# Attention heads in the middle of a unit: mixing of one head and scores of another move into a unit of matrix products, and two engines take up a new order

## The chip, the cores and the metric

The kernel runs on one core of a Trainium2 chip. The metric is the time of one execution on the device in microseconds (us), lower is better. Shown are the median of three runs and one execution taken by the hardware profiler.

The engines by their short names: PE is TensorE (matrix products; PEld is its loading of weights), DVE is VectorE, ACT is ScalarE, POOL is GpSimd, SP is SyncE, which here only issues DMAs. Each engine works off its own instructions in the order in which they are written, and waits on semaphores for the others.

## The reference

One token block of 512 positions with 1024 channels goes through a convolutional block with a gated feed-forward part, a retention layer with its feed-forward part, an attention layer, and a last feed-forward part. Only attention matters here: 16 heads of 64 channels. A chunk of 64 queries sees its own chunk and all earlier ones in the block (eight at most).

```python
def _chunk_attention(h, w_in, rel_bias, w_out):
    q, k, v = jnp.split(h @ w_in, 3, axis=-1)
    ...
        s = jnp.einsum('bqhd,bkhd->bhqk', qb, kb).astype(jnp.float32) * scale + bias[None]
        s = jnp.where(valid[None, None, None, :], s, -jnp.inf)
        p = jax.nn.softmax(s, axis=-1).astype(vb.dtype)
        return jnp.einsum('bhqk,bkhd->bqhd', p, vb)
    ...
    return o @ w_out
```

## The kernel before

**Units.** All big products are done in units of 24 matrix products (unit8, unit4, unit_v): each operand is split in a high and a low part, and a product is the sum of three (L686, L687, L688: high by high, low by high, high by low in some order). ACT makes the high part of weights (a half block at a time, L1200, in convert_half), POOL the low part (L665), SP loads the raw weights. A unit starts when its weights are ready (w_lo) and when its PSUM bank has been emptied (unit_taken); at its end it raises unit_done. In attention only banks 0 and 1 hold units (banks[0] = 2), since the others hold scores, turned probabilities and the mixture.

**The attention loop** runs over heads h = 1 to 15 on PE, ACT and DVE, each with its own copy of the loop. Queries, keys and values of four heads (a group) come from six units, done while other heads are worked on: qk_unit(0) to qk_unit(3) (queries and keys of two heads each) and two unit_v. With s = h % 4, head h has unit_v and qk_unit(0) at s = 1, qk_unit(1) at s = 2, qk_unit(2) at s = 3, qk_unit(3) and unit_v at s = 0. In the last group of heads (13 to 15, last_group) the units are parts of the output projection (unit4_narrow), which use both banks at a time.

**One head's way.** scores(h) on PE (L1057, L1059; four tiles of queries by their keys, in banks 2, 3 and 6) raises scores_done. maxima(h) on DVE adds the bias and takes row maxima (L2410), raising s_taken, then negates them (L2414). exps(h) on ACT (L1616) makes exponentials and row sums, and issues the DMA of the bias of h + 4 (load_bias). normalise(h) on DVE (L2418, L2423) divides, raising p_ready. turn(h) on PE (L1075) transposes ten blocks of probabilities into banks 4, 5 and 6; bank 6 also holds a tile of scores, so its two blocks wait until maxima(h + 1) have read it. probs_hi(h) on ACT (L1625) and probs_lo(h) on DVE (L2429) take the high and low parts, raising pt_ready. mix(h) on PE (L1086, L1088) multiplies by the values into bank 7; it waits for pt_ready of its own head and for mix_added of the head before. mixed_copy and mixed_hi on ACT (L1631, L1636), mixed_add and mixed_lo on DVE (L2434, L2440) bring the mixture into two parts for the output projection. The last tile of scores(h) waits for pt_ready of head h - 2, whose turned blocks stood in bank 6.

**Queries and keys.** After a qk_unit DVE scales it (qk_taken, L2006), ACT takes the high part (qk_hi, L1580 and L1581), DVE the low part (qk_lo, L2400). ACT then converts some halves of weights (qk_done: one, none, two, one for the four units) and, for keys, issues two DMAs that copy the high part to the other half of the partitions (copy_k_hi, L1587), for which its queue first waits for its own high part. SP does the same for the low part.

**Order.** It is written out by hand for each engine and each s. On PE, at s = 1, 2 and 3: the unit, scores(h + 1), mix(h - 1), turn(h); at s = 0: qk_unit(3), unit_v, scores(h + 1), mix(h - 1), turn(h). On ACT and DVE the work on the unit comes first, that on head h + 1 next, the parts of head h behind it.

Of the kernel before, what the change touches and what calls it, by code (L numbers as in the profile page):

```python
# [26 lines left out]
D = 1024  # L27
# [137 lines left out]
def build(nc, phases, x_in, w_in, w_out, w_gate, w_up, w_down, ret_w_in, ret_w_out, att_w_in,  # L165
# [4 lines left out]
    with ctx:  # L170
# [45 lines left out]
        sq, sq_end, so_far = cols[:, 32:36], cols[:, 36:40], cols[:, 40:44]  # L216
# [463 lines left out]
        def _(pe):  # L680
# [36 lines left out]
            def unit4(rhs, k0, ready=None, fresh=1, bank0=None, last=None):  # L717
# [7 lines left out]
                for m, k in [(m, k) for tiles in ((0, 1, 2), (3,)) for m in range(2) for k in tiles]:  # L725
                    if ready and m == 0:
                        pe.wait_ge(ready, c.next(ready))
# [194 lines left out]
            for f in phases:  # L922
# [107 lines left out]
                if f == "att":  # L1030
# [7 lines left out]
                    def unit4_narrow(n):  # L1038

                        unit4(H, 0, fresh=0, bank0=0)  # L1040
# [64 lines left out]
                    for h in range(1, ATT_HEADS):  # L1105
                        s, last_group = h % 4, h >= ATT_HEADS - 4
                        if s == 0:
                            qk_unit(3)
                            unit_v(X)
                            scores(h + 1)  # L1110
                            mix(h - 1)
                            turn(h)
                            continue
# [3 lines left out]
                        if last_group and s == 1:  # L1117
                            scores(h + 1)
                            pe.wait_ge(mix_ready, 8)
                            unit4_narrow(s - 1)  # L1120
                        else:
                            if last_group:
                                unit4_narrow(s - 1)
                            else:
                                qk_unit(s - 1)
                            if h + 1 < ATT_HEADS:
                                scores(h + 1)
                        if s == 1:
                            pe.wait_ge(unit_taken, v_units)
                        mix(h - 1)  # L1130
# [12 lines left out]
        def _(act):  # L1143
# [224 lines left out]
            for f in phases:  # L1368
# [197 lines left out]
                if f == "att":  # L1566
# [89 lines left out]
                    for h in range(1, ATT_HEADS):  # L1656
                        s, last_group = h % 4, h >= ATT_HEADS - 4
                        if s == 0:
                            qk_unit(3)
                            mixed_copy(h - 1)  # L1660
                            v_unit(0)
                            exps(h + 1)
# [5 lines left out]
                        if last_group and s == 1:  # L1668
                            exps(h + 1)
                            after_unit()  # L1670
                            mixed_copy(h - 1)
                        else:
                            if last_group:
                                after_unit()
                            else:
                                qk_unit(s - 1)
                            mixed_copy(h - 1)
                            if h + 1 < ATT_HEADS:
                                exps(h + 1)
                        probs_hi()  # L1680
# [12 lines left out]
        def _(dve):  # L1693
# [207 lines left out]
            def end_rows(u):  # L1901
# [10 lines left out]
                if u == 12:  # L1912
                    ended(1, right)
                    dve.wait_ge(squared, 4)
                    V.tensor_scalar(so_far[:, 2:4], sq[:, 2:4], 1.0 / D, EPS, ALU.mult, ALU.add).then_inc(dve_step, c.made(dve_step))
                    dve.wait_ge(dve_step, c.now(dve_step))
                if u in (12, 13):
# [4 lines left out]
                    V.tensor_scalar(ms[:, p:p + 1], sq_end[:, p:p + 1], 1.0 / D, so_far[:, p:p + 1], ALU.mult, ALU.add).then_inc(  # L1922
# [114 lines left out]
            for f in phases:  # L2037
# [333 lines left out]
                if f == "att":  # L2371
# [99 lines left out]
                    for h in range(1, ATT_HEADS):  # L2471
                        s, last_group = h % 4, h >= ATT_HEADS - 4
                        if s == 0:
# [3 lines left out]
                            mixed_add(h - 1)  # L2477
                            value_lo()
                            normalise(h + 1)
# [5 lines left out]
                        if last_group and s == 1:  # L2485
                            maxima(h + 1)
                            out_narrow(s - 1)
                            mixed_add(h - 1)
                            normalise(h + 1)
                        elif last_group:  # L2490
                            out_narrow(s - 1)
                            if h + 1 < ATT_HEADS:
                                maxima(h + 1)
                            mixed_add(h - 1)
                            if h + 1 < ATT_HEADS:
# [72 lines left out]
```

## Time and profile before

| | |
|---|---|
| median of three runs | 1866.5 us (1863.9 to 1867.17) |
| the profiled execution | 1866.14 us, its span 1864.3 us |
| PE busy | 1841.6 us, 99% |
| DVE, POOL, ACT busy | 1133.3 us (61%), 944.8 us (51%), 843.2 us (45%) |
| attention loop, heads 1 to 15 | 1315.6 to about 1499 us of the span |
| mean granted clock of PE | 0.997 of full speed |

The span goes from the first to the last instruction. A timeline line gives start, duration, engine and line; x10 means ten instructions merged; a bracket gives the idle time in front of it and what ended it. The durations of PE's products overlap, since they are pipelined: the time that one takes of the engine is the distance to the next start, 0.23 us for 512 columns and 0.12 us for 256.

### The profile page before, as it was taken

How to read it: one execution, taken by the hardware profiler on the slowest of the kernel's cores; microseconds unless marked ns; L12 is line 12 of the kernel's file. 1: busy time of each engine (PE TensorE's matmuls, PEld its weight loads, DVE VectorE, ACT ScalarE, POOL GpSimd, SP SyncE). 2: the span in 40 equal slices, each digit the busy share in tenths (PEclk: the TensorE clock that was granted, in tenths of full speed). 3: DMA queues.
4: the chain of work that ended last, by engine and by line, in shares of the span. 5: the costliest groups of instructions: out<-in, count | busy, mean ns of one | idle time of the engine just before them, and what ended most of it. 6: DMA issues, size and time to landing. Idle time of an engine off the chain costs nothing.

```text
span 1864.3 us, 24027 instructions
## 1 busy us (share of the span) xinstructions
PE 1841.6 (99%) x9444; PEld 1570.6 (84%) x9444; DVE 1133.3 (61%) x1816; ACT 843.2 (45%) x1318; POOL 944.8 (51%) x407
## 2 busy tenths in 40 slices
PE   8999999999999999999999999999999999999998
PEld 7778889898888888888889898998888887888886
DVE  6987775775776333343565445457777766454546
ACT  5335443343354233332454445355666646443544
POOL 5673466475443433333448566574222327674755
PEclk9999999999999999999999999999999999999999
DMA  5222414424232222222243232403333332423221
GB/s 186 91 91 68 140 64 141 158 69 158 73 113 68 91 91 87 72 91 90 75 174 114 68 136 67 137 25 100 98 103 111 103 98 83 136 76 127 91 91 57
DMA packets 142764, 187.10 MB, mean 100 GB/s; under 512 B 4000, under 2 KB 102576, under 8 KB 142528
## 3 DMA queue, kind: packets, MB, share of 16 engines
q1 hardware_dynamic: 134848, 171.72, 27.9%
q10 hardware_dynamic: 7808, 13.91, 2.6%
q8 instruction: 72, 1.18, 0.3%
q14 instruction: 36, 0.29, 0.0%
HBM read 179.28 MB, written 6.33 MB: 100 GB/s over the span
## 4 chain that ended last, share of the span: by engine, by line
PE 81%; DVE 8%; ACT 3%; POOL 1%; issue 1%; ACTq 0%; DVEq 0%
PE ps L686 26%; PE ps L687 26%; PE ps L688 26%; DVE ps L2068 1%; POOL w_lo L665 1%; ACT w_hi L1200 1%; DVE diagonals L1736 1%; DVE xl L1762 0%; ACT work L1616 0%; DVE probs_t_lo L2429 0%; PE ps L1075 0%; DVE work L2423 0%; PE ps L1009 0%; DVE work L2410 0%; DVE work L2006 0%
## 5 line engine op out<-in xcount | busy, mean ns | idle before, releaser
L665 POOL TENSOR_TENSOR w_lo<-raw,w_hi 128x1024 fp32r<-128x1024 f32 x244 | 590.9, 2430 | 755.5 <-ACT w_hi L1200 755.4
L686 PE MATMUL ps<-xh,w_hi 128*128 128x512 f32 x1408 | 555.1, 394 | 5.7 <-DVE xl L1762 3.5
L688 PE MATMUL ps<-xh,w_lo 128*128 128x512 f32 x1408 | 549.3, 390 | 0.0
L687 PE MATMUL ps<-xl,w_hi 128*128 128x512 f32 x1408 | 549.1, 390 | 0.0
L1200 ACT ACTIVATE w_hi<-raw 128x1024 fp32r<-128x1024 f32 x262 | 273.2, 1057 | 426.3 <-PE ps L688 397.6
L686 PEld LDWEIGHTS ps<-xh,w_hi 128*128 128x128 f32 x1408 | 265.0, 188 | 65.0 <-issue 10.1
L687 PEld LDWEIGHTS ps<-xl,w_hi 128*128 128x128 f32 x1408 | 265.1, 188 | 55.5 <-issue 1.9
L688 PEld LDWEIGHTS ps<-xh,w_lo 128*128 128x128 f32 x1408 | 264.9, 188 | 55.5
L686 PE MATMUL ps<-hid_hi,w_hi 128*128 128x256 f32 (+1 forms) x688 | 228.4, 332 | 1.5 <-DVE hid_lo L2012 0.7
L688 PE MATMUL ps<-hid_hi,w_lo 128*128 128x256 f32 (+1 forms) x688 | 227.1, 330 | 0.0
L687 PE MATMUL ps<-hid_lo,w_hi 128*128 128x256 f32 (+1 forms) x688 | 227.1, 330 | 0.0
L686 PEld LDWEIGHTS ps<-hid_hi,w_hi 128*128 128x128 f32 x688 | 130.8, 190 | 14.6 <-DVE hid_lo L2012 1.8
L688 PEld LDWEIGHTS ps<-hid_hi,w_lo 128*128 128x128 f32 x688 | 130.8, 190 | 12.1
L687 PEld LDWEIGHTS ps<-hid_lo,w_hi 128*128 128x128 f32 x688 | 130.9, 190 | 11.7 <-issue 0.2
L665 POOL TENSOR_TENSOR w_lo<-down,w_hi 128x1024 fp32r<-128x1024 f32 x40 | 96.2, 2420 | 84.0 <-ACT w_hi L1200 84.0
L1977 DVE TENSOR_TENSOR x<-x,ps 128x512 f32<-128x512 f32 x84 | 56.9, 684 | 75.5 <-PE ps L688 75.5
L665 POOL TENSOR_TENSOR w_lo<-work,w_hi 128x1024 fp32r<-128x1024 f32 x36 | 86.3, 2413 | 13.0 <-ACT w_hi L1200 13.0
L2344 DVE SCALAR_TENSOR_TENSOR work<-ps,r_bc 128x512 f32<-128x512 f32 x64 | 43.6, 689 | 79.6 <-PE ps L688 79.6
L686 PE MATMUL ps<-w_hi,xh 128*128 128x512 f32 (+1 forms) x256 | 86.6, 338 | 0.7 <-DVE work L2229 0.7
L687 PE MATMUL ps<-w_lo,xh 128*128 128x512 f32 (+1 forms) x256 | 86.0, 336 | 0.0
L688 PE MATMUL ps<-w_hi,xl 128*128 128x512 f32 (+1 forms) x256 | 86.0, 336 | 0.0
L688 PE MATMUL ps<-combined,w_lo 128*128 128x256 f32 x288 | 81.5, 283 | 0.0
(272 smaller groups left out, 3095.0 us busy)
## 6 DMA issues: line engine op xcount, KB each, us to landing
raw<-in_mlp_w_dram SPq DMA_DIRECT2D x40, 1024.0 KB, 5.5
raw<-in_ret_w_in_dram SPq DMA_DIRECT2D x24, 1024.0 KB, 5.2
work<-in_mlp_w_dram SPq DMA_DIRECT2D x16, 1024.0 KB, 5.7
raw<-in_att_w_in_dram SPq DMA_DIRECT2D x12, 1024.0 KB, 5.3
raw<-in_w_gate_dram SPq DMA_DIRECT2D x11, 1024.0 KB, 5.3
raw<-in_w_up_dram SPq DMA_DIRECT2D x11, 1024.0 KB, 5.4
raw<-in_w_in_dram SPq DMA_DIRECT2D x9, 1024.0 KB, 5.1
raw<-in_ret_w_out_dram SPq DMA_DIRECT2D x8, 1024.0 KB, 5.0
```

The lines of the kernel that those rows point to most:

```text
L665: nc.gpsimd.tensor_tensor(half_of(wl[:, b % 2, :], b, half), half_of(source, b, half), half_of(wh[:, b % 2, :], b, half).bitcast(F32), ALU ...
L686: nc.tensor.matmul(o, a[0], b[0], start=first, stop=False, skip_group_check=True)
L687: nc.tensor.matmul(o, a[0], b[1], start=False, stop=False, skip_group_check=True)
L688: return nc.tensor.matmul(o, a[1], b[0], start=False, stop=last, skip_group_check=True)
L1200: nc.scalar.activation(to, source, ACT.Copy).then_inc(w_hi, c.made(w_hi))
L1736: V.reciprocal(rough, root_rows).then_inc(dve_step, c.made(dve_step))
L1977: V.tensor_tensor(tiles, tiles, ps[:, where, :].rearrange("p (m c) -> p m c", m=2), ALU.add).then_inc(unit_taken, c.made(unit_taken))
L2068: V.scalar_tensor_tensor(total if last else acc, src, w, acc, ALU.mult, ALU.add).then_inc(signal, c.made(signal))
L2344: V.scalar_tensor_tensor(hval[:, u % 2, :], bank(), 0.0, r_bc[:, :], ALU.max, ALU.mult).then_inc(unit_taken, c.made(unit_taken))
```

## The change

- unit4 and unit4_narrow take a function that is called in the middle of the unit, as unit8 has already. It is called ahead of the fifth of eight triples of products.
- PE: at s = 1, 2 and 3, mix(h - 1) goes into the middle of the unit, and so does scores(h + 1) at s = 1 (except in the last group) and s = 2, behind mix. At s = 3 scores(h + 1) stays behind the unit. At s = 0 mix(h - 1) and scores(h + 1), now in this order, go between qk_unit(3) and unit_v.
- ACT: mixed_copy(h - 1) goes first. Exponentials of h + 1 go ahead of the work on the unit at s = 1 and 2; at s = 1 probs_hi(h) too goes ahead of it. At s = 0 the exponentials go ahead of the values' part. The last group gets a corresponding order.
- DVE: at s = 1 and 2, maxima(h + 1) and mixed_add(h - 1) go ahead of qk_taken, and probs_lo(h) ahead of normalise(h + 1). At s = 3 the order is mixed_add, qk_taken, maxima, qk_lo, normalise, probs_lo. At s = 0 normalise(h + 1) goes ahead of value_lo.
- A name of a small tile (so_far) becomes sq_half; its three places are left out below.

```diff
@@ -714,7 +714,7 @@
                 mm.then_inc(unit_done, c.made(unit_done))
                 c.unit.n += 1
 
-            def unit4(rhs, k0, ready=None, fresh=1, bank0=None, last=None):
+            def unit4(rhs, k0, ready=None, fresh=1, bank0=None, last=None, between=None):
 
                 slot, half = c.unit.n // 2 % 2, c.unit.n % 2
                 pe.wait_ge(w_lo, low(1))
@@ -723,6 +723,8 @@
                 w = weights(slot, 512)
 
                 for m, k in [(m, k) for tiles in ((0, 1, 2), (3,)) for m in range(2) for k in tiles]:
+                    if between and (m, k) == (1, 1):
+                        between()
                     if ready and m == 0:
                         pe.wait_ge(ready, c.next(ready))
                     if last and (m, k) == (0, 3):
@@ -1035,9 +1037,9 @@
                         slot0 = (c.unit.n - n) // 2 % 2
                         unit8(X, slot=(slot0 + n % 2) % 2, half=n // 2, ahead=(1, 2, 0, 1)[n], between=between)
 
-                    def unit4_narrow(n):
-
-                        unit4(H, 0, fresh=0, bank0=0)
+                    def unit4_narrow(n, between=None):
+
+                        unit4(H, 0, fresh=0, bank0=0, between=between)
 
                     def scores(h):
 
@@ -1106,9 +1108,9 @@
                         s, last_group = h % 4, h >= ATT_HEADS - 4
                         if s == 0:
                             qk_unit(3)
+                            mix(h - 1)
+                            scores(h + 1)
                             unit_v(X)
-                            scores(h + 1)
-                            mix(h - 1)
                             turn(h)
                             continue
                         if s == 1 and h > 1:
@@ -1116,18 +1118,21 @@
                             v_units = c.unit.n
                         if last_group and s == 1:
                             scores(h + 1)
+
+                        def inside():
+                            if s == 1:
+                                pe.wait_ge(unit_taken, v_units)
+                            mix(h - 1)
+                            if s == 2 or s == 1 and not last_group:
+                                scores(h + 1)
+
+                        if last_group:
                             pe.wait_ge(mix_ready, 8)
-                            unit4_narrow(s - 1)
+                            unit4_narrow(s - 1, inside)
                         else:
-                            if last_group:
-                                unit4_narrow(s - 1)
-                            else:
-                                qk_unit(s - 1)
-                            if h + 1 < ATT_HEADS:
+                            qk_unit(s - 1, inside)
+                            if s == 3:
                                 scores(h + 1)
-                        if s == 1:
-                            pe.wait_ge(unit_taken, v_units)
-                        mix(h - 1)
                         turn(h)
                     unit4_narrow(3)
                     mix(ATT_HEADS - 1)
@@ -1658,26 +1663,31 @@
                         if s == 0:
                             qk_unit(3)
                             mixed_copy(h - 1)
+                            exps(h + 1)
                             v_unit(0)
-                            exps(h + 1)
                             probs_hi()
                             mixed_hi(h - 1)
                             continue
                         if s == 1 and h > 1:
                             v_unit(1)
-                        if last_group and s == 1:
+                        if last_group:
+                            if s == 1:
+                                exps(h + 1)
+                            mixed_copy(h - 1)
+                            if s == 2:
+                                exps(h + 1)
+                            after_unit()
+                            probs_hi()
+                        else:
+                            mixed_copy(h - 1)
+                            if s == 3:
+                                qk_unit(2)
                             exps(h + 1)
-                            after_unit()
-                            mixed_copy(h - 1)
-                        else:
-                            if last_group:
-                                after_unit()
-                            else:
-                                qk_unit(s - 1)
-                            mixed_copy(h - 1)
-                            if h + 1 < ATT_HEADS:
-                                exps(h + 1)
-                        probs_hi()
+                            if s == 2:
+                                qk_unit(1)
+                            probs_hi()
+                            if s == 1:
+                                qk_unit(0)
                         mixed_hi(h - 1)
                     after_unit()
                     mixed_copy(ATT_HEADS - 1)
@@ -2475,35 +2485,40 @@
                             maxima(h + 1)
                             qk_lo(3)
                             mixed_add(h - 1)
+                            normalise(h + 1)
                             value_lo()
-                            normalise(h + 1)
                             probs_lo()
                             mixed_lo(h - 1)
                             continue
                         if s == 1 and h > 1:
                             value_lo()
-                        if last_group and s == 1:
-                            maxima(h + 1)
-                            out_narrow(s - 1)
-                            mixed_add(h - 1)
-                            normalise(h + 1)
-                        elif last_group:
-                            out_narrow(s - 1)
-                            if h + 1 < ATT_HEADS:
+                        if last_group:
+                            if s < 3:
                                 maxima(h + 1)
                             mixed_add(h - 1)
-                            if h + 1 < ATT_HEADS:
+                            if s == 1:
                                 normalise(h + 1)
+                            out_narrow(s - 1)
+                            probs_lo()
+                            if s == 2:
+                                normalise(h + 1)
+                        elif s == 3:
+                            mixed_add(h - 1)
+                            qk_taken(2)
+                            maxima(h + 1)
+                            qk_lo(2)
+                            normalise(h + 1)
+                            probs_lo()
                         else:
+                            maxima(h + 1)
+                            mixed_add(h - 1)
                             qk_taken(s - 1)
-                            maxima(h + 1)
                             if s == 2:
-                                qk_lo(s - 1)
-                            mixed_add(h - 1)
-                            if s != 2:
-                                qk_lo(s - 1)
+                                qk_lo(1)
+                            probs_lo()
                             normalise(h + 1)
-                        probs_lo()
+                            if s == 1:
+                                qk_lo(0)
                         mixed_lo(h - 1)
                     out_narrow(3)
                     mixed_add(ATT_HEADS - 1)
```

## Rows read from the trace of the kernel before

**Rows 1.** The page, part 1: busy us, share of the span, instructions.

```profile
PE 1841.6 (99%) x9444; PEld 1570.6 (84%) x9444; DVE 1133.3 (61%) x1816; ACT 843.2 (45%) x1318; POOL 944.8 (51%) x407
```

**Rows 2.** Waits of PE, 1315 to 1500 us: total, times, longest.

```profile
PE ps L1075 <- DVE cols L2410: 2.4, 7, 0.5
PE ps L1057 <- DVE probs_t_lo L2429: 0.7, 2, 0.4
```

**Rows 3.** Timeline of PE: start, us, operation [idle before it, and releaser].

```profile
1321.13 0.22 PE L1057 MATMUL ps<-k_parts,q_hi 128*128 128x128 f32 x1
...
1322.63 0.38 PE L1057 MATMUL ps<-k_parts,q_hi 128*128 128x256 f32 x1 [0.30 <-DVE probs_t_lo L2429]
...
1322.97 0.40 PE L1086 MATMUL ps<-probs_t_hi,att_v 128*128 128x512 f32 x1
...
1324.20 1.28 PE L1075 MATMUL ps<-ident,work 128*128 128x128 f32 x10
1325.23 0.47 PE L686 MATMUL ps<-xh,w_hi 128*128 128x512 f32 x1
...
1330.80 0.22 PE L1057 MATMUL ps<-k_odd,q_lo 128*128 128x128 f32 x1
...
1350.99 0.28 PE L686 MATMUL ps<-w_hi,xh 128*128 128x256 f32 x1
...
1356.75 0.22 PE L1057 MATMUL ps<-k_odd,q_lo 128*128 128x128 f32 x1
```

**Rows 4.** Timeline of ACT, 1322 to 1336 us.

```profile
1323.21 0.63 ACT L1580 ACTIVATE q_hi<-work 64x512 fp32r<-64x512 f32 x1 [2.45 <-DVE work L2006]
...
1324.51 1.06 ACT L1200 ACTIVATE w_hi<-raw 128x1024 fp32r<-128x1024 f32 x1
1325.59 0.59 ACT L1631 ACTIVATE work<-ps 64x512 f32<-64x512 f32 x1
...
1328.32 0.19 ACT L1616 ACTIVATION_READ_ACCUMULATOR work<-work,cols 128x1 f32 x1
1328.53 1.36 ACT L1625 ACTIVATE probs_t_hi<-ps 128x512 fp32r<-128x512 f32 x3
...
1335.47 0.62 ACTq L1587 DMA_DIRECT2D k_odd<-k_odd  x1
```

**Rows 5.** Timeline of DVE, 1320 to 1333 us.

```profile
1320.97 1.61 DVE L2429 TENSOR_TENSOR probs_t_lo<-ps,probs_t_hi 128x512 fp32r<-128x512 f32 x3
1322.50 0.68 DVE L2006 SCALAR_TENSOR_TENSOR work<-ps,r_bc 128x512 f32<-128x512 f32 x1
1323.10 0.28 DVE L2410 CUSTOM_DVE_ANT_0 work<-ps,work 128x128 f32<-128x128 f32 x1
...
1324.85 0.17 DVE L2414 TENSOR_SCALAR cols<-cols 128x4 f32<-128x4 f32 x1
1326.22 0.68 DVE L2434 TENSOR_TENSOR work<-ps,work 64x512 f32<-64x512 f32 x1 [1.20 <-ACT work L1631]
1326.93 1.67 DVE L2400 TENSOR_TENSOR q_hi<-work,q_hi 64x512 fp32r<-64x512 f32 x1
1328.63 0.69 DVE L2400 TENSOR_TENSOR q_lo<-work,q_lo 64x512 fp32r<-64x512 f32 x1
...
1329.57 1.28 DVE L2423 TENSOR_SCALAR work<-work,cols 128x128 f32<-128x128 f32 x4
1330.76 1.61 DVE L2429 TENSOR_TENSOR probs_t_lo<-ps,probs_t_hi 128x512 fp32r<-128x512 f32 x3
```

**Rows 6.** Timeline of POOL, 1320 to 1330 us.

```profile
1325.64 2.42 POOL L665 TENSOR_TENSOR w_lo<-raw,w_hi 128x1024 fp32r<-128x1024 f32 x1 [6.10 <-ACT w_hi L1200]
```

**Rows 7.** Two stretches: length, busy us by engine, granted clock, DMA, GB/s.

```profile
core 0: us, PE busy (x) PEld busy (x) DVE busy (x) ACT busy (x) POOL busy (x), PEclk, DMA share, GB/s
8.41:15.24 6.83, 5.45 (x13) 4.20 (x14) 4.32 (x6) 6.06 (x11) 4.14 (x3) 0.50 0.99 333
1855.00:1858.40 3.40, 1.78 (x8) 1.13 (x6) 2.87 (x10) 1.28 (x4) 0.00 (x0) 1.00 0.55 223
```

**Rows 8.** Timeline of PE, 6 to 11 us.

```profile
9.79 0.77 PE L686 MATMUL ps<-xh,w_hi 128*128 128x512 f32 x1 [3.51 <-DVE xl L1762]
```

More of the change, by code:

```diff
@@ L215, in build @@
         mv = cols[:, 24:32].rearrange("p (i c) -> p i c", c=2)
-        sq, sq_end, so_far = cols[:, 32:36], cols[:, 36:40], cols[:, 40:44]
+        sq, sq_end, sq_half = cols[:, 32:36], cols[:, 36:40], cols[:, 40:44]
         mx, nmx, rs, rinv = (cols[:, 32 + 4 * k:36 + 4 * k] for k in range(4))
@@ L1914, in end_rows @@
                     dve.wait_ge(squared, 4)
-                    V.tensor_scalar(so_far[:, 2:4], sq[:, 2:4], 1.0 / D, EPS, ALU.mult, ALU.add).then_inc(dve_step, c.made(dve_step))
+                    V.tensor_scalar(sq_half[:, 2:4], sq[:, 2:4], 1.0 / D, EPS, ALU.mult, ALU.add).then_inc(dve_step, c.made(dve_step))
                     dve.wait_ge(dve_step, c.now(dve_step))
@@ L1921, in end_rows @@
                     dve.wait_ge(squared, p + 3)
-                    V.tensor_scalar(ms[:, p:p + 1], sq_end[:, p:p + 1], 1.0 / D, so_far[:, p:p + 1], ALU.mult, ALU.add).then_inc(
+                    V.tensor_scalar(ms[:, p:p + 1], sq_end[:, p:p + 1], 1.0 / D, sq_half[:, p:p + 1], ALU.mult, ALU.add).then_inc(
                         to_curve, c.made(to_curve))
```

## The prediction, made before the change was run

> **What bounds the kernel now.** I read the page first, then the waits of TensorE (PE), then the timelines of the four engines over one head of attention. PE is busy for 99% of the span [rows 1]. So nothing can be gained by doing other engines' work faster. What can be gained or lost is PE's idle time. The attention loop runs from 1315.6 to about 1499 us. In its wait table the longest kinds are the turning products L1075 waiting for the last row maximum (2.4 us, 7 times) and the last score product L1057 waiting for low parts of the probabilities (0.7 us, 2 times) [rows 2]. The table counts idle from a modelled end, which lies 0.17 us after the time at which the next product could have started, so each of these waits costs that much more: the 0.30 us before the product at 1322.63 is a gap of 0.47 between starts [rows 3]. Summed over the 15 such gaps from 1315 to 1499 us I get about 6.5 us. That is all that any reordering of this loop can win: 0.35% of the time.
>
> **Who feeds PE.** Head h goes through this ring: scores (PE), maxima (DVE), exponentials (ACT), normalising (DVE), turning (PE), high part (ACT), low part (DVE), mixing (PE). In the kernel before, a whole unit of other products stands between turning head h-1 and the first need of its low parts. I call the first half of a unit H. A unit with its ten turning products takes 6.60 us (1324.20 to 1330.80), and turning alone about 1.06, so a unit is 5.5 us and H is 2.73. A values' unit takes 5.76 (1350.99 to 1356.75). Scores take 1.3 to 1.4 undisturbed (1.84 from 1321.13 to 1322.97 less the gap; I use 1.27, as where nothing waits), mixing 1.23 (1322.97 to 1324.20) [rows 3].
> Even with the whole unit the cover is thin: turning of head 1 ends at 1325.23, its low parts are done at 1332.37 (1330.76 plus 1.61), 7.1 us later [rows 3, 5].
>
> **What the change does to that cover.** Mixing of h-1 moves from behind the unit (and behind the scores) into its middle. It now comes H, 2.73 us, after turning of h-1, where it came 5.5 + 1.3 = 6.8 us after it. The low parts took 7.1 us. So the new order on ACT and DVE must bring them forward by 4.4 us. Whether it does must be laid out head by head, with these durations. ACT [rows 4]: exponentials of a head 2.3 (from the end of the mixture's copy at 1326.18 to 1328.51), high parts 1.36, a part of queries or keys 1.3 (1323.21 to 1324.51, two of 0.63), a converted half of weights 1.0 (1.06 with its tail), copy of the mixture 0.6, and on keys' units 1.2 in which ACT's queue issues two DMAs of about 0.6 each and lets nothing pass (the second from 1335.47 to 1336.09). DVE [rows 5]: maxima 1.75 and their negation 0.17, normalising 1.4 with its reciprocal, low parts 1.55, scaling a unit 0.62, a low part of queries or keys two times 0.70, sum of the mixture 0.7. PE to the next engine and back cost 0.05 to 0.2 each.
>
> **The lock between POOL and DVE.** The low part of the queries at 1326.93 takes 1.67 us where the next, of the same form, takes 0.69. POOL ran its product of weights from 1325.64 to 1328.06, and the DVE instruction ended 0.54 us after that [rows 5, 6]. So an instruction of DVE that reads SBUF alone waits out a POOL instruction of 2.4 us; those that read PSUM (scaling, maxima, low parts) don't. I use this for normalising and for the low parts of queries and keys. The Trainium skill ("SBUF — State Buffer", section "SBUF: two separate sides") states it as an exclusive lock of the shared port pair, held for the whole instruction; by that rule normalising is locked out too, which no row of mine shows at full length. Without any lock the layout below comes to +16.7 us, with it to +27.7.
>
> **The layout.** I put the four queues in the order of the code with these numbers. As a test I did it first for the kernel before: mixing of head 15 ends at 1498.4 by the layout and at about 1499 in the trace, with 7.7 us of stalls where the gaps give 6.5. For the changed order, zero at the end of turning of a head with h%4 = 1:
> - h%4 = 2. PE: H to 2.7; mixing finds its low parts (DVE done at 2.5), no wait; scores to 5.2, second half to 8.0. DVE: low parts to 2.5, normalising to 3.9, low part of queries: one half to 4.6, then POOL has the port (4.6 to 7.0), other half to 7.7, low part of the mixture to 8.35. Only then come the maxima of h+1, whose scores were there at 5: 8.35 to 10.1. The last two turning products wait for them: 1.3 us. Turning ends at 10.3.
> - h%4 = 3. ACT: exponentials 10.3 to 12.6, then, ahead of the turned parts, keys' part to 13.9 and its DMA issues to 15.0, high parts to 16.4. DVE: low parts at 17.2. PE wanted them at 10.3 + 2.7 = 13.1: a stall of 4.2 us. Then mixing, half, scores to 22.5, and 0.5 us for the maxima; turning ends at 24.0.
> - h%4 = 0. ACT: queries' part to 23.4, two converted halves to 25.4, exponentials to 27.6, high parts to 29.0. POOL holds the port from 27.8 to 30.1. DVE: normalising to 31.3 and only behind it low parts to 32.9. PE has done its unit at 29.5: a stall of 3.5 us. Before, a values' unit and the scores stood here too, another 7 us of cover.
> - h%4 = 1. A values' unit and H lie between: no wait.
> Per group of four heads 1.3 + 4.2 + 0.5 + 3.5 = 9.5 us, three groups 28 (the first 0.4 less). Head 1: mixing of head 0 now comes at 1318.1, its low parts, whose order is untouched, at 1322.58 [rows 5]: 4.5. Last group, narrow units: 2.9, since each waits for both banks of the one before. In all 35.4 against 7.7 laid out for before: **+27.7 us**. The gaps that the change is to close (maxima before turning, scores before low parts) are in that sum: they shrink or vanish in places, and cost more at h%4 = 2.
> Exchanging names (so_far) costs nothing. No instruction is added. SP's queue keeps its order; its waits on the low parts of keys come a few us later in a group of now 58, and each load had over 10 us in hand. The POOL queue also keeps its order.
>
> **The clock.** All of the loop runs at full level. In this trace PE idled once for as long as these stalls: 3.51 us before the product at 9.79 [rows 8]. Around it the granted clock is 0.50 (1.2 GHz) from 8.41 to 15.24 us, with 5.45 us of PE work in it [rows 7]; at full level that is half, so the fall cost 2.7 us. At the end of the kernel, in a stretch in which PE worked 1.78 of 3.40 us, it stayed at 1.00 [rows 7]. The long stalls laid out above, 3.5 to 4.5 us, are thus of the one length ahead of which a fall is on record. I price one fall from nothing (it comes at the end of a stall and part of it is taken up by the next stall) to 2.7 us, and take 2 us, nearer to the row. All eight would give about +14 (two of them are half taken up), four give +8.
> The Trainium skill ("TensorE: Matmul & The Clock Gate", "Why this matters for your kernels") likewise warns of idle gaps between bursts of products. By its words all stalls of this length are at risk; the trace has the one case, and the sum needs only that.
>
> **The rivals.**
> - A, forecast: the stalls come and the clock falls at about half of the long ones: 1866.1 + 27.7 + 8 = 1902, from 1896 to 1909. Chance 0.55.
> - B: the stalls come, the clock holds: 1893.8. For it: each stall hardly exceeds the one seen. Chance 0.22.
> - C: POOL's lock doesn't hit normalising and the keys' parts where I put it: +16.7, so 1883 with the clock held. For it: the order of POOL and DVE hangs on tenths. Against: low parts of queries are hit in every group before. Chance 0.10.
> - D, the other side: ACT and DVE do bring the low parts within 2.73 us of turning, so mixing never waits, and the maxima are ready for turning. Then up to 6.5 us are won: 1860. The point from which it decides is ACT's: exponentials of the next head must be done before turning begins, at h%4 = 3 too. At h%4 = 1 to 2 this holds; at 3 the keys' part and 1.17 us of DMA issues stand ahead of the high parts. Chance 0.07.
> - E: the waits only change places and the sum stays within 0.2% of before, about 1866. That would also be so if the halves inside a unit did not cut as the code says. Chance 0.04.
> - More than A's upper end (all falls, each at 2.7 us, or other engines slowed too): 0.02.
>
> **Numbers.** All sums start from the profiled run, 1866.14 us, of which 1864.3 is span; it is 0.4 below the median of three, 1866.5, so the forecast needs no shift. 1883 to 1911 holds A, B and C, and leaves out D, E and a little above. 0.2%, 3.7 us, is about what a measurement of this kernel can tell from no change. Faster by more: D, 0.07. Within: E, 0.04. Slower by more: the rest, 0.89.
>
> **What would show it.** In the profile after: L1086 (mixing) appears as a waiter for DVE's low parts L2429 (by its new number), with some 25 us in all and single waits of 3.5 to 4.5; the wait of L1075 for maxima stays near 1 us at h%4 = 2; the loop from head 1 to head 15 lengthens by 28 to 42 us and nothing outside it; the granted clock has stretches of 0.50 behind long stalls. Rival B shows the same waits and a clock of 1.00, C waits near 2 us, D none on L1086. I am wrong in the mechanism if PE never waits for L2429 in the middle of a unit, and wrong in size if the stall at h%4 = 0 is missing, because normalising got the port first.

## The result, and the profile after

The changed kernel takes 1908.2 us (median; 1905.5 to 1909.1) against 1866.8 of the kernel before on the same chip: a ratio of 1.0225, 95% interval 1.0212 to 1.0237. The profiled execution took 1909.05 us (span 1907.3), 42.9 us more than the profiled one before.

The page of the kernel after, busy time and the granted clock over 40 slices (compare [rows 1]):

```profile
PE 1858.0 (97%) x9444; PEld 1583.8 (83%) x9444; DVE 1142.4 (60%) x1816; ACT 841.9 (44%) x1318; POOL 946.5 (50%) x407
PEclk9999999999999999999999999999899999999999
```

PE has the same 9444 instructions, but 16.4 us more busy time: some of them ran slower. The one 8 in the clock's row, the slice from 1478 to 1526 us, points at one such place; the others hardly show in slices of 47.7 us. Idle and slower work are two separate losses, and each has its own view.

Waits of PE in the kernel after, 1300 to 1550 us, total, times, longest (compare [rows 2]):

```profile
PE ps L1088 <- DVE probs_t_lo L2439: 24.8, 7, 4.2
PE ps L1077 <- DVE cols L2420: 3.2, 7, 0.7
PE ps L686 <- DVE x L2459: 1.8, 4, 0.8
PE ps L686 <- DVE att_v L2393: 0.7, 1, 0.7
```

A new first row: mixing (now L1088) waits seven times for low parts of the probabilities. The sum is 30.5 us in 19 waits; with 0.17 us for each, as in the prediction, 33.7. Before it was 6.5, so the stalls cost **27.2 us**. Turning still waits for the maxima seven times, 3.2 us in all where it was 2.4.

Timeline of PE after, the instructions behind a stall of over 0.3 us in the first group of heads (compare [rows 3]):

```profile
1323.25 0.62 PE L1088 MATMUL ps<-probs_t_hi,att_v 128*128 128x512 f32 x1 [4.16 <-DVE probs_t_lo L2439]
...
1340.88 0.44 PE L1077 MATMUL ps<-ident,work 128*128 128x128 f32 x2 [0.52 <-DVE cols L2420]
...
1348.18 0.77 PE L1088 MATMUL ps<-probs_t_hi,att_v 128*128 128x512 f32 x1 [4.10 <-DVE probs_t_lo L2439]
...
1357.71 0.44 PE L1077 MATMUL ps<-ident,work 128*128 128x128 f32 x2 [0.36 <-DVE cols L2420]
...
1366.41 0.47 PE L1088 MATMUL ps<-probs_t_hi,att_v 128*128 128x512 f32 x1 [2.78 <-DVE probs_t_lo L2439]
```

These are head 1, then h%4 = 2, 3 and 0. The pattern comes back at 1409 and 1428, and at 1471 and 1487.

Why it waits at 1348.18 (ACT, then DVE, kernel after): exponentials end at 1343.3, keys' part and its DMA issues follow, and only then the high parts of the turned probabilities.

```profile
1343.27 0.61 ACT L1585 ACTIVATE k_parts<-work 64x512 fp32r<-64x512 f32 x1
1343.89 0.63 ACT L1586 ACTIVATE k_odd<-work 64x512 fp32r<-64x512 f32 x1
1344.60 0.48 ACTq L1592 DMA_DIRECT2D k_parts<-k_parts  x1
1345.12 0.62 ACTq L1592 DMA_DIRECT2D k_odd<-k_odd  x1
1345.78 1.36 ACT L1630 ACTIVATE probs_t_hi<-ps 128x512 fp32r<-128x512 f32 x3 [1.27 <-issue]
...
1346.41 1.62 DVE L2439 TENSOR_TENSOR probs_t_lo<-ps,probs_t_hi 128x512 fp32r<-128x512 f32 x3 [0.46 <-ACT probs_t_hi L1630]
...
1348.15 1.27 DVE L2433 TENSOR_SCALAR work<-work,cols 128x128 f32<-128x128 f32 x4
```

And at 1366.41 (POOL, ACT, DVE): the high parts began at 1361.47 and took 1.36 us, but DVE normalises first, and that takes 3.04 us here where it takes 1.27 in the row above, with POOL busy from 1358.40 to 1363.66.

```profile
1358.40 5.26 POOL L665 TENSOR_TENSOR w_lo<-raw,w_hi 128x1024 fp32r<-128x1024 f32 x2 [20.48 <-ACT w_hi L1205]
...
1361.47 1.36 ACT L1630 ACTIVATE probs_t_hi<-ps 128x512 fp32r<-128x512 f32 x3
...
1361.69 3.04 DVE L2433 TENSOR_SCALAR work<-work,cols 128x128 f32<-128x128 f32 x4
1364.66 1.61 DVE L2439 TENSOR_TENSOR probs_t_lo<-ps,probs_t_hi 128x512 fp32r<-128x512 f32 x3
```

The second loss. The seven stretches of the loop of the kernel after in which the granted clock is 0.50 (columns as in [rows 7]), the first, second and last of them and the sum of all seven:

```profile
1323.40:1326.81 3.41, 3.41 (x13) 3.22 (x14) 0.00 (x0) 0.59 (x1) 0.00 (x0) 0.50 0.35 118
1347.30:1354.13 6.83, 5.95 (x17) 5.01 (x18) 3.46 (x9) 1.09 (x2) 0.00 (x0) 0.50 0.16 38
...
1487.25:1494.08 6.83, 6.63 (x25) 6.27 (x26) 3.92 (x14) 3.58 (x7) 2.38 (x1) 0.50 0.17 40
sum 34.12, PE 32.00 PEld 28.93 DVE 17.18 ACT 11.65 POOL 5.05; mean PE 4.57 PEld 4.13 DVE 2.45 ACT 1.66 POOL 0.72
```

Each begins within 1.5 us of the end of one of the seven long stalls. PE did 32.0 us of work in them, which takes half as long at the full level: **16.0 us** lost. 27.2 + 16.0 = 43.2, against 42.9 measured.

### The profile page after: what moved, and what is told of

It is laid out like the page before. It is cut to its first block, busy times and chain, and to the rows that moved or that the text cites. A ratio compares the mean times of both kernels' runs of the same rounds, so it can differ in the third digit from the quotient of the medians.

```text
span 1907.3 us, 24027 instructions
## 1 busy us (share of the span) xinstructions
PE 1858.0 (97%) x9444; PEld 1583.8 (83%) x9444; DVE 1142.4 (60%) x1816; ACT 841.9 (44%) x1318; POOL 946.5 (50%) x407
## 4 chain that ended last, share of the span: by engine, by line
PE 79%; DVE 9%; ACT 4%; issue 2%; POOL 1%; ACTq 0%; DVEq 0%
PE ps L686 25%; PE ps L687 25%; PE ps L688 25%; DVE ps L2078 1%; ACT work L1621 1%; POOL w_lo L665 1%; ACT w_hi L1205 1%; DVE probs_t_lo L2439 1%; DVE work L2420 1%; DVE work L2433 1%; PE ps L1088 1%; DVE diagonals L1746 1%; PE ps L1090 1%; DVE xl L1772 0%; PE ps L1011 0%
```

## The experiments

The theory: the low parts come late for three separate reasons (ACT's order at h%4 = 3, DVE's order and POOL at h%4 = 0, the untouched order of head 0), and each long stall costs its length and a fall of the clock. The rivals: the clock's part is something else, such as slower products by conflicts; POOL's hold on DVE doesn't matter; the loss is the work of one engine's order alone.

**1. Fill the stalls.** Ahead of mixing's wait PE does unused products; the operands and the other engines' orders stay.

```diff
+FILL = {0: 14, 2: 14, 6: 14, 10: 14, 3: 10, 7: 10, 11: 10}
...
+                        for _ in range(FILL.get(h, 0)):
+                            nc.tensor.matmul(ps[:, 7, :], X[0][:, 0, 0:P], X[0][:, 0, :], start=True, stop=True, skip_group_check=True)
```

> The changed kernel with 14 or 10 products of 512 columns (0.2275 us each) put ahead of the wait for low parts at the seven long stalls (mixing of heads 0, 2, 6, 10: 14; of 3, 7, 11: 10). They write into the mixture's bank, which the next product overwrites, and stand in time that PE would have idled. Theory (stalls by waits for DVE 27.7 us, and a lower clock behind each): no stretch at half level in the loop, waits of L1088 fall to about 1 us each, the waits of DVE and ACT stay where they are, time 1866.8 + 27.7 = 1894.5, from 1892 to 1897; so the clock's part is 14 us. Rival (the half level is a mere sign of the stalls and costs nothing, since other engines end last there): the clock is full and the time stays at 1908. Second rival (PE's speed does not matter and the filling gets in the way): over 1908.

Measured: 1894.3 us, ratio 1.0150 (1.0133 to 1.0167). Waits of PE in this kernel, 1300 to 1550 us, then its stretch from 1315 to 1500 us, which is most of the loop, then the same stretch of the kernel after:

```profile
PE ps L1091 <- DVE probs_t_lo L2442: 4.8, 7, 0.9
```

```profile
1315.00:1500.00 185.00, 176.10 (x1026) 153.23 (x1025) 137.74 (x306) 103.01 (x233) 49.75 (x20) 1.00 0.28 84
```

```profile
1315.00:1500.00 185.00, 156.97 (x849) 137.01 (x847) 126.97 (x283) 94.87 (x216) 45.50 (x18) 0.91 0.28 82
```

The clock stays at 1.00, where it was 0.91, and no stretch of the loop is at half level. Late data cost as much as before, since the fill only takes the place of idle time, but 13.9 us are gone. That is the clock's part, net; what is left over the kernel before, 27.9 us, is the stalls' part.

**2 to 4. Undo two causes, one by one and together.** In the second, at h%4 = 2 (where the low parts that mixing will want at h%4 = 3 are made), the parts of h go ahead of the keys' part on ACT and DVE. In the third, at h%4 = 3, DVE's low parts go ahead of normalising.

```diff
@@ second: ACT, then DVE (s = 2)
-                            if s == 2:
-                                qk_unit(1)
                             probs_hi()
-                            if s == 1:
-                                qk_unit(0)
+                            if s < 3:
+                                qk_unit(s - 1)
...
+                            probs_lo()
                             if s == 2:
                                 qk_lo(1)
-                            probs_lo()
@@ third: DVE (s = 3)
-                            normalise(h + 1)
                             probs_lo()
+                            normalise(h + 1)
```

> The changed kernel, with the high parts of the turned probabilities ahead of the keys' part and its DMA issues on ACT at h%4 = 2, and the low parts ahead of the keys' low part on DVE. Theory (the stall at h%4 = 3 is ACT's 1.3 us of keys' part and 1.2 us of DMA issues ahead of the high parts): each of the three stalls there falls from 4.2 to about 1.7 us, turning at h%4 = 3 waits 0.4 more, stalls in all -6 us, and three falls of the clock go too: 1908.2 - 6 - 5 = 1897, from 1893 to 1901. Rival (the exponentials of the next head alone set it, the rest is hidden): stalls stay at 4.2 and the time at 1908.

> The changed kernel, with the low parts ahead of normalising on DVE at h%4 = 3. Theory (the stall at h%4 = 0 is DVE's normalising ahead of the low parts, held up by POOL's hold on the port): the three stalls of 2.9 us there fall to under 0.5, their three falls of the clock go, 1908.2 - 9 - 5 = 1894, from 1890 to 1898. Rival (ACT's high parts, behind two conversions and the exponentials, set it): the stalls stay above 2 us, the time falls by less than 3 us.

> Both edits. Theory: the savings add up; left over are the stall of head 1 (4.5 us, with a fall of the clock), three of 1.7 us at h%4 = 3 and those for the maxima: 12.3 us over the kernel before by stalls, 14 with the clock: 1881, from 1877 to 1885. Rival (one stall's time is only handed to the next): not below 1890.

Measured: 1899.3 us (1.0178; 1.0161 to 1.0195), 1894.5 (1.0154; 1.0137 to 1.0171), and both 1884.9 (1.0099; 1.0083 to 1.0116). The stall that each takes away, in the timelines of PE of the second and of the third:

```profile
1345.75 0.47 PE L1088 MATMUL ps<-probs_t_hi,att_v 128*128 128x512 f32 x1 [1.71 <-DVE probs_t_lo L2437]
```

```profile
1362.36 0.47 PE L1088 MATMUL ps<-probs_t_hi,att_v 128*128 128x512 f32 x1 [0.27 <-DVE probs_t_lo L2439]
```

4.10 became 1.71, and 2.78 became 0.27. With the stalls went most of the falls: seven in the kernel after, five in the second (one of them behind the 1.71 us shown), four in the third, and one with both. The two gains, 8.9 and 13.7 us, add up to 22.6, and together they gave 23.3. With both, though, 1885 was at the slow end of what was expected (1877 to 1885), and the timeline shows two waits in the first group that neither edit alone leaves (what makes them was not followed up):

```profile
1352.32 0.30 PE L1059 MATMUL ps<-k_parts,q_hi 128*128 128x128 f32 x1 [1.00 <-issue]
...
1362.53 0.47 PE L1088 MATMUL ps<-probs_t_hi,att_v 128*128 128x512 f32 x1 [1.57 <-DVE probs_t_lo L2437]
```

**5 and 6. Take POOL's hold away.** In the kernel after (5) and in the one before (6), POOL makes the low part of the attention weights for one of eight blocks of columns only; seven eighths of these low parts are left out, PE's work is the same.

```diff
+                    low, source, high = [half_of(t, b, half) for t in (wl[:, b % 2, :], source, wh[:, b % 2, :])]
+                    if in_att:
+                        low, source, high = [t[:, 0:1, :] for t in (low, source, high)]
```

> The changed kernel with POOL's low parts of the weights of queries, keys and values in attention cut to one of 8 rows of blocks (a product over 128 instead of 1024 columns), so those low parts are left out for seven eighths and POOL holds the port for some tenths of a us instead of 2.4. Theory (POOL's hold on the port of DVE is what delays the maxima at h%4 = 2 and normalising at h%4 = 0): the waits for maxima vanish at h%4 = 2, the stalls at h%4 = 0 fall from 2.9 to about 1.2, those at h%4 = 3 from 4.2 to about 2.7; head 1 stays. 12 us over the kernel before by stalls, and fewer falls of the clock: 1883, from 1878 to 1890. Rival (DVE's long instructions have another cause, POOL runs beside them by chance): times as in the changed kernel, 1908, or over 1900.

> The same cut in the kernel before, as the measure for the run above. Theory: the waits for low parts at heads 1 and 2 and for the maxima get shorter: 1866.4 - 4.5 = 1862, from 1860 to 1865. Rival (no hold on the port): 1866 as before.

Measured: 1882.8 us (1.0094; 1.0079 to 1.0110) and 1860.2 (0.9973; 0.9962 to 0.9984). In the fifth, POOL's instruction and the waits of PE (total, times, longest):

```profile
1358.36 0.46 POOL L669 TENSOR_TENSOR w_lo<-raw,w_hi 128x128 fp32r<-128x128 f32 x1 [8.36 <-ACT w_hi L1207]
```

```profile
PE ps L1090 <- DVE probs_t_lo L2441: 13.9, 7, 2.9
```

So the change costs 22.6 us where POOL's instructions are short, and 41.3 where each takes 2.4 us. Nearly half of the loss is late orders meeting POOL. Three falls were left.

Head 1 was expected to stay and did not: its stall fell from 4.16 to 2.47 us. Ahead of the low parts of head 0, for which that mixing waits, stand the maxima, exponentials and normalising of head 1, and the negation of these maxima takes 1.82 us in the kernel after, beside POOL (1315.32 to 1320.05 us), and 0.17 in the fifth run:

```profile
1315.90 1.82 DVE L2424 TENSOR_SCALAR cols<-cols 128x4 f32<-128x4 f32 x1
...
1312.93 0.17 DVE L2426 TENSOR_SCALAR cols<-cols 128x4 f32<-128x4 f32 x1
```

So the third of the causes named above is in part POOL's hold too.

**7 and 8. One side of the change alone.** Seven: the new order of ACT and DVE with PE's old one. Eight: PE's new order with the old one of ACT and DVE. The core of each, against the kernel after:

```diff
@@ seven: PE
-                            mix(h - 1)
-                            scores(h + 1)
                             unit_v(X)
+                            scores(h + 1)
+                            mix(h - 1)
...
-                            qk_unit(s - 1, inside)
+                                qk_unit(s - 1)
...
+                        mix(h - 1)
@@ eight: ACT
+                                qk_unit(s - 1)
...
-                            exps(h + 1)
-                            if s == 2:
-                                qk_unit(1)
-                            probs_hi()
-                            if s == 1:
-                                qk_unit(0)
+                                exps(h + 1)
+                        probs_hi()
```

> The new order of ACT and DVE with TensorE's order of the kernel before: the whole unit and the scores stand again between turning and mixing. Nothing of the computation is left out. Layout: the low parts still come late by the rows of the changed kernel (keys' part and its DMA issues ahead of the high parts at h%4 = 3, normalising ahead of the low parts at h%4 = 0), but now the cover is longer, so the long waits of mixing for low parts go; in their place the maxima come late (waits of up to 3 us of turning at h%4 = 2 and 3) because the unit's own scaling and parts come in another order than PE delivers. Sum of stalls by layout +27.5 us, and two or three falls of the clock: 1894 to 1898 us. Rival, that only TensorE's order matters and ACT's and DVE's order is an improvement on any order of TensorE: 1866 or less.

> The kernel before with PE's new order alone; ACT and DVE keep their old order. Theory (the new order on ACT and DVE does bring the low parts forward, only not enough): now 13 to 14 long stalls of 1.7 to 4.5 us, at h%4 = 2 too, since exponentials and normalising stand ahead of the low parts at every head; 55 us by stalls and some 12 to 20 by the clock: 1935, from 1920 to 1945. Rival (the reordering of ACT and DVE is what hurts, PE's is harmless): below 1885.

Measured: seven 1902.9 us (1.0202; 1.0187 to 1.0218), eight 1944.9 (1.0423; 1.0407 to 1.0439). Waits of PE in seven, then in eight, 1300 to 1550 us:

```profile
PE ps L1077 <- DVE cols L2417: 17.1, 7, 2.9
PE ps L686 <- DVE x L2456: 8.9, 4, 5.2
```

```profile
PE ps L1088 <- DVE probs_t_lo L2434: 39.9, 10, 4.5
PE ps L1077 <- DVE cols L2415: 11.1, 10, 1.6
```

Neither half is harmless: +37 and +79 us. With the old order on ACT and DVE, PE's new one stalls in most heads; the new order on ACT and DVE brings the waits for low parts from 39.9 to 24.8 us and those for maxima from 11.1 to 3.2 (to the end of the eighth run's longer loop they are 43.0 and 13.2). By itself, beside PE's old order, it makes the maxima late. Seven was expected at 1894 to 1898. Its stalls are as laid out (26.9 us by the gaps, laid out 27.5); its clock fell seven times and not two or three, and cost some 10 us (11.6 by the windows). Eight ended at the upper end of its 1920 to 1945, for the same reason: its stalls are 56.0 us by the gaps, laid out 55, but the clock fell eleven times and cost 23.6 us by the windows, where 12 to 20 were expected.

**9. A better order by the layout.** A search over the orders, costed with the same durations, gave this one (PE keeps the whole unit before mixing at h%4 = 1 to 3 and splits the values' unit at h%4 = 0; letters are the steps: t scaling, x maxima, ma sum of the mixture, q low parts of the unit, w values' part, ml its low part, n normalising, p low parts):

```diff
+DVE_STEPS = {0: 't x ma q w ml n p'.split(), 1: 'w x p ma t n ml q'.split(), 2: 't x ma q n ml p'.split(), 3: 't x ma q p ml n'.split()}
```

> An order that keeps a whole unit between turning of a head and its mixing, and uses the middle of a unit only where low parts have had 5.5 us: at h%4 = 0 mixing and scores in the middle of the values' unit; scores inside or behind as before elsewhere, at h%4 = 2 behind mixing. On ACT and DVE the parts of head h go ahead of the exponentials and the normalising of h+1 at h%4 = 1, 3. Theory (PE's idle time of 6.5 us in the loop is all there is to win): the waits left are 0.7 at head 1, 0.5 three times for the maxima and 0.6 for the first narrow unit: 1866.4 - 5 = 1861.4, from 1860 to 1864. Rival (PE's gaps are a fixed cost of its semaphores, and go nowhere): 1866.

Measured: 1870.7 us (1.0028; 1.0017 to 1.0038), a miss by 9 us, to the other side. POOL, DVE and PE of this kernel:

```profile
1332.67 2.39 POOL L669 TENSOR_TENSOR w_lo<-raw,w_hi 128x1024 fp32r<-128x1024 f32 x1 [11.83 <-ACT w_hi L1211]
...
1332.00 0.69 DVE L2400 TENSOR_TENSOR q_hi<-work,q_hi 64x512 fp32r<-64x512 f32 x1
1332.72 2.89 DVE L2400 TENSOR_TENSOR q_lo<-work,q_lo 64x512 fp32r<-64x512 f32 x1
...
1338.03 0.69 PE L1083 MATMUL ps<-ident,work 128*128 128x128 f32 x2 [2.35 <-DVE cols L2410]
```

POOL started 0.05 us before DVE's second low part, in the gap between two DVE instructions; that one took 2.89 us instead of 0.69, the maxima came late, and turning waited 2.35 us. The same happened in all three groups (POOL ahead by 0.05 or 0.06 us each time), and behind the first of them the clock fell once. The layout, which gave the maxima 0.5 us, did not have this hold.

**10. A robust order.** PE: mixing ahead of scores at h%4 = 2, both inside the values' unit at h%4 = 0, otherwise as before. DVE: low parts ahead of normalising in every head before the last group. ACT: high parts ahead of exponentials only at h%4 = 2. The copy of the mixture at h%4 = 2 and 3 and the values' low part at h%4 = 0 change places too. It was chosen as the one whose sum stays good when single durations are moved by tenths.

```diff
-                            unit_v(X)
-                            scores(h + 1)
-                            mix(h - 1)
+                            unit_v(X, both)
...
+                            if s == 2 and not last_group:
+                                mix(h - 1)
```

> TensorE keeps the order of the kernel before, but for mixing ahead of scores at h%4 = 2, and mixing and scores in the middle of the values' unit at h%4 = 0. DVE takes the low parts of the probabilities ahead of normalising in every head, ACT takes the high parts ahead of exponentials at h%4 = 2 only. Nothing of the computation is left out. Layout: 3.5 us less of stalls than in the kernel before (2.3 to 4.4 when single durations are moved by tenths), with no stall over 1.1 us and so no fall of the clock: 1862.8 us, from 1861.5 to 1864.5. Rival, that such orders hang on tenths in which POOL and DVE take the port and that the layout can't see them (as in the run e9_parts_first): a wait of 2 us for the maxima in each group, 1866 to 1872.

Measured: 1862.3 us, ratio 0.9983 (0.9974 to 0.9992): the one full version that beats both kernels, by 0.17%. Its maxima before turning:

```profile
PE ps L1077 <- DVE cols L2425: 1.5, 4, 0.5
```

Four waits are left of the seven of [rows 2]. No stretch of the loop has a half clock. Its profiled execution (1864.4 us) shows only 1.7 us of the gain, the medians 3.9; the interval (1.5 to 4.9 us) holds both.

**11. The ninth with short POOL products** (the same seven eighths of low parts left out; the edit is that of 5), to test what was said of the ninth.

> The order of e9_parts_first, with POOL's low parts of the attention weights taken over 128 of 1024 columns, so that this part of the weights' low parts is left out of the computation. If the 10 us by which e9_parts_first missed its layout are POOL holding the port in front of DVE's second low part of the queries, they go: 1861 us (1859 to 1863), the waits of turning L1083 for the maxima fall from 7.4 us to under 2 us, and no stretch of the loop has a half clock. The kernel before with the same short products took 1860.2. Rival, that the 2.4 us waits come from the order itself: 1868 to 1871 with the waits still there.

Measured: 1861.5 us (0.9972; 0.9962 to 0.9982). Waits of PE:

```profile
PE ps L1085 <- DVE cols L2412: 1.6, 4, 0.4
```

Of the 7.4 us that turning waited in the ninth, 1.6 are left: the rest was POOL. And both orders, the old one (1860.2) and this one, are then 1.3 us apart, to the old one's side: this order has no gain of its own.

## Why the prediction was right, and where it was not

It said 1902.0 us, from 1883 to 1911; the median is 1908.2. The case that came is A, stalls and falls of the clock, within its own range (1896 to 1909).

- **What bounds the kernel.** Right. PE's idle time (27.2) and its time at half clock (16.0), both inside the loop, are all of the 42.9 us.
- **The cover** of 2.73 us instead of 6.8 before the low parts are wanted: right, as the first row of the waits after and the eighth run show.
- **The layout**, as gaps (bracket plus 0.17), predicted and measured: head 1 4.5 and 4.33; h%4 = 3 4.2 and 4.27; h%4 = 0 3.5 and 2.95; maxima at h%4 = 3 0.5 and 0.53; last group 2.9 and 3.4 (1.8 and 0.7 us in five waits). Too high: the maxima at h%4 = 2, 1.3 against 0.69 (0.88 in the second group). Sum +27.7 predicted, +27.2 from the waits, +27.9 from the first experiment. That the sum is this close is partly luck: the layout had 35.4 for 33.7 us after and 7.7 for 6.5 before, and the two errors cancel. The loop lengthened by 43.0 us (the first product behind mixing of head 15 starts at 1499.25 and 1542.24), a little over the 28 to 42 named, and nothing outside it did.
- **The stall at h%4 = 0** was laid out 0.5 us too long. The half clock is not the reason: in the first experiment, all at full level, PE does unused products from 1360.00 on and mixing starts at 1362.88, so the stall is 2.88 us there too.

```profile
1360.00 2.43 PE L1086 MATMUL ps<-xh 128*128 128x512 f32 x10
...
1362.88 0.50 PE L1091 MATMUL ps<-probs_t_hi,att_v 128*128 128x512 f32 x1 [0.45 <-DVE probs_t_lo L2442]
```

  What differs first is POOL: in the layout it holds the port until 6.1 us after the end of turning and the low parts are done at 8.9; in the kernel after, where turning ends at 1357.90, POOL ends at 5.8 and the low parts at 8.4.
- **POOL and DVE.** This was the assumption without a full-length row, and rival C was its absence. The normalising of 3.04 us is that row, and the fifth and sixth runs price all of POOL's holds together: without them the change costs 22.6 us, near C's 16.7 plus three falls (the gaps of the two runs differ by 16.3). The hold at head 1, 1.82 against 0.17 us, was not seen in the prediction; it got the stall right because it took that time from the trace of before, where it is as long. The Trainium skill ("SBUF — State Buffer", section "SBUF: two separate sides") has the port pair held for a whole instruction; these rows agree, 2.89 us of DVE against 2.39 of POOL in the ninth run.
- **The clock: the term that was mis-sized.** The prediction took four falls at 2 us, +8. There were seven, one behind each long stall, with 16.0 us lost by the windows and 13.9 net by the first experiment: 2.0 to 2.3 us each. The price per fall was right, the number was not. The text had "all eight would give about +14", and took half only because one stall of that length [rows 8] was all it had. The forecast with all falls would have been 1908. The Trainium skill ("TensorE: Matmul & The Clock Gate", "Why this matters for your kernels") warns of idle gaps between bursts of products. It would have pointed to a fall behind each of the four stalls of 4 us, and the trace agrees; a fall came behind each of the three of 2.78 us too.
- **Rivals.** B (the clock holds, 1893.8) is what the first experiment built on purpose: 1894.3. D, the gain, would need high parts ahead of the keys' part and low parts ahead of normalising; the fourth run has both and still loses 18.6 us, with stalls of 4.16 us at head 1 and of 1.7 at h%4 = 3 left. Its turning point was put at ACT's order alone, which was one of at least three.

Not separated by a run: how much of head 1's 2.47 us that are not POOL's hold an order of its own for head 0 would save.

## What to carry to other kernels

When the engine that is busy 99% of the time gets a consumer moved nearer to its producer, lay out the producer's whole chain, engine by engine, before believing in it: the cover lost (here 4 us per head) is paid in full wherever the chain's order isn't shortened by as much. Then price every stall of 2.7 us and more twice, once for its length and once for the slower products behind it. And where a gain hangs on which of two engines takes a shared port first by tenths of a microsecond, take the order that is good either way, even if its layout looks 1 us worse.

## What the runs showed of the hardware that was not expected

- **Falls of the clock by the stall before them**, over the kernel after and experiments 2 to 5, 7 to 9: 35 waits of PE of 2.7 us or more, and 34 had a stretch of clock 0.50 that began within 1.5 us of their end; seven of 2.1 to 2.5 us, of which four had one; 18 of 1.2 to 1.9 us, of which one had (1.71 us, in the second run). The exception and a shorter one, in the seventh run: first PE behind a wait of 2.73 us that ended at 1337.13, then behind one of 2.26 that ended at 1345.27.

```profile
1337.00:1340.40 3.40, 3.27 (x16) 2.76 (x17) 1.62 (x5) 3.08 (x10) 0.00 (x0) 1.00 0.27 72
1346.02:1349.43 3.41, 3.41 (x14) 3.02 (x13) 0.38 (x1) 0.00 (x0) 0.00 (x0) 0.50 0.02 5
```

  The half level lasted 3.41 or 6.83 us each time; what decides between the two was not tried.
- **DVE doesn't keep the port between two of its own instructions.** In the ninth run POOL got in between two that followed each other by 0.72 us from start to start, and held the second up by 2.2 us. A small instruction is held as well: the negation over 128x4, 0.17 us by itself, took 1.82 at head 1 beside POOL.
- **The layout's size is good, its order at ties is not.** With durations from one trace it gave the stalls of the kernel after and of the seventh run within 1 us of the 27 measured, and missed the ninth by 9 us, most of it because of one tie per group, decided by 0.05 or 0.06 us.
